# The low half of every weight, made on VectorE or on GpSimd

## The reference

```python
for layer in range(DEPTH):                      # DEPTH = 2
    h = rms_norm(x, mix_norm_g[layer])
    y = hgrn2_mixer(...) if layer % 2 == 0 else mla_mixer(...)
    m = memory_attention(...)
    x = x + concatenate([y, m]) @ w_out[layer]
    x = x + conv_ffn(rms_norm(x, ffn_norm_g[layer]), w_up[layer], ..., w_down[layer])
h = x
h = h + 0.5 * _swiglu(_rmsnorm(h, ffn1_norm), ffn1_w_in, ffn1_w_out)
z = _rmsnorm(h, mix_norm) @ w_in
h = h + concatenate([_conv_module(...), _gla(...)]) @ w_out
h = h + 0.5 * _swiglu(_rmsnorm(h, ffn2_norm), ffn2_w_in, ffn2_w_out)
h = h + sigmoid(_rmsnorm(h, ple_norm) @ ple_w_gate) * (p @ ple_w_proj)
return _rmsnorm(h, final_norm)
```

## Time and profile before

| | |
|---|---|
| median of 3 runs | 1320.73 us |
| span of the profiled execution | 1316.1 us |
| its own time | not on the page; by the median 4.6 us lie around the span |
| TensorE busy | 1248.9 us, 95% |
| VectorE busy | 844.6 us, 64% |
| ScalarE busy | 662.6 us, 50% |
| GpSimd busy | 3.5 us |
| mean granted TensorE clock | 0.978 |

### The profile page before, as it was taken

How to read it: one execution, slowest core, us unless ns; L and a number is a source line. 1 busy time by engine, 2 the same in 40 slices (tenths; PEclk the granted TensorE clock), 3 DMA queues, 4 the chain that set the end, 5 groups by cost and what they waited for, 6 DMA issues and landing times.

```text
span 1316.1 us, 21598 instructions
## 1 busy us (share of the span) xinstructions
PE 1248.9 (95%) x8351; PEld 1140.8 (87%) x8360; DVE 844.6 (64%) x1556; ACT 662.6 (50%) x1156; POOL 3.5 (0%) x9
## 2 busy tenths in 40 slices
PE   6999789999999889999999999999999899999996
PEld 6999768999998667899999799999899679999984
DVE  7877947666667845666766655554778855555563
ACT  6745435555546643555555534443667134344452
POOL 0000000000000000000000000000000000000000
PEclk9999979999999979999999999999999999999998
DMA  8534403554455212255455454455543134444540
GB/s 346 199 134 145 147 30 144 191 191 182 175 188 207 111 49 96 101 201 184 186 191 192 147 207 179 185 191 191 189 148 144 49 120 183 176 178 183 189 144 32
DMA packets 20433, 211.40 MB, mean 161 GB/s; under 512 B 2400, under 2 KB 2400, under 8 KB 3360
## 3 DMA queue, kind: packets, MB, share of 16 engines
q1 hardware_dynamic: 20016, 208.90, 42.9%
q0 software_dynamic: 368, 1.84, 0.4%
HBM read 209.68 MB, written 1.05 MB: 160 GB/s over the span
## 4 chain that ended last, share of the span: by engine, by line
PE 86%; DVE 8%; ACT 4%; issue 1%; DMA 1%; SPq 0%; ACTq 0%; DVEq 0%
PE ps L305 25%; PE ps L306 25%; PE ps L307 25%; PE ps L310 10%; DVE w_lo L1233 2%; ACT w_hi L812 1%; ACT arena L812 1%; DMA raw<-in_stream 1%; ACT arena L847 1%; DVE x L1299 1%; DVE arena L1729 0%; PE ps L633 0%; PE ps L468 0%; DVE arena L1323 0%; DVE arena L1547 0%
## 5 line engine op out<-in xcount | busy, mean ns | idle before, releaser
L1233 DVE TENSOR_TENSOR w_lo<-raw,w_hi 128x1024 fp32r<-128x1024 f32 (+1 forms) x390 | 444.7, 1167 | 41.3 <-ACT w_hi L812 40.6
L305 PE MATMUL ps<-h_hi,w_hi 128*128 128x256 f32 x1608 | 456.0, 284 | 0.2 <-DVE h_lo L1286 0.2
L307 PE MATMUL ps<-h_hi,w_lo 128*128 128x256 f32 x1608 | 455.0, 283 | 0.0
L306 PE MATMUL ps<-h_lo,w_hi 128*128 128x256 f32 x1608 | 455.0, 283 | 0.0
L812 ACT ACTIVATE w_hi<-raw 128x1024 fp32r<-128x1024 f32 (+1 forms) x390 | 379.1, 1007 | 6.0 <-PE ps L307 4.6
L305 PEld LDWEIGHTS ps<-h_hi,w_hi 128*128 128x128 f32 x1608 | 308.3, 192 | 3.5 <-issue 0.3
L306 PEld LDWEIGHTS ps<-h_lo,w_hi 128*128 128x128 f32 x1608 | 308.3, 192 | 3.2
L307 PEld LDWEIGHTS ps<-h_hi,w_lo 128*128 128x128 f32 x1608 | 308.3, 192 | 0.0
L305 PE MATMUL ps<-w_hi,y_hi 128*128 128x512 f32 (+2 forms) x550 | 212.1, 386 | 12.3 <-DVE y_lo L1342 5.0
L306 PE MATMUL ps<-w_lo,y_hi 128*128 128x512 f32 (+2 forms) x550 | 210.4, 382 | 0.0
L307 PE MATMUL ps<-w_hi,y_lo 128*128 128x512 f32 (+2 forms) x550 | 209.3, 381 | 0.0
(11 more groups left out here) (275 smaller groups left out, 1037.9 us busy)
## 6 DMA issues: line engine op xcount, KB each, us to landing
raw<-in_stream SPq DMA_DIRECT2D x130, 1536.0 KB, 6.3
x<-in_x SPq DMA_DIRECT2D x1, 1024.0 KB, 4.9
arena<-in_mem SPq DMA_DIRECT2D x1, 1024.0 KB, 11.9
x<-in_x POOLq DMA_DIRECT2D x1, 1024.0 KB, 5.7
out<-arena SPq DMA_DIRECT2D x4, 256.0 KB, 2.5
vec<-in_vectors SPq DMA_DIRECT2D x1, 893.0 KB, 6.6
arena<-in_final POOLq DMA_DIRECT2D x1, 512.0 KB, 5.6
arena<-in_masks SPq DMA_DIRECT2D x1, 352.0 KB, 12.0
```

The costliest lines, as they stand in the source:

```text
L305: pe.matmul(o, lh, rh, start=start, stop=False, skip_group_check=True)
L306: pe.matmul(o, lh, rl, start=False, stop=False, skip_group_check=True)
L307: return pe.matmul(o, ll, rh, start=False, stop=stop, skip_group_check=True)
L1233: dve.tensor_tensor(w_lo[:, s, a], raw[:, s, a], w_hi[:, s, a], ALU.subtract).then_inc(s_lo, 1)
```

## The change

GpSimd gets a helper `split`, and makes the low part of all 390 pieces in the order of the stream: those of units 0 to 5, then it sets the area of line 287 to zero (for which it waits as before), then those of units 6 to 129. All calls of `lo` and `split` on VectorE go, and with them the arguments `between` and `after` of two helpers. Since GpSimd works its queue in order, the three transfers move to ScalarE's queue: x behind the copy of the queries of the first memory attention, the other two between the sums of squares and the rest of the norm ahead of the last feed-forward part. No wait of TensorE, SyncE or ScalarE on a counter is changed.

```diff
@@ block.gpsimd
             pool.memset(zero[:, :], 0.0).then_inc(sem("zero_set"), 1)
 
+            def split(units):
+                for u in units:
+                    s = u % SLOTS
+                    for p in range(3):
+                        a = extent(u, p)
+                        pool.wait_ge(s_hi, 3 * u + p + 1)
+                        pool.tensor_tensor(w_lo[:, s, a], raw[:, s, a], w_hi[:, s, a],
+                                           ALU.subtract).then_inc(s_lo, 1)
+
+            split(range(0, U_I))
             pool.wait_ge(sem("memT_lo_done"), 2)
             pool.memset(A(4608, HEADS * S), 0.0).then_inc(sem("r_zero"), 1)
-
-            pool.wait_ge(sem("hg_o_ready"), 1)
-            pool.wait_ge(sem("ma_qT_ready"), 1)
-            pool.dma_start(x[:, :, :], x_in).then_inc(sem("x_back"), 16)
-
-            pool.wait_ge(sem("x_done"), 4 * 6)
-            pool.dma_start(ple, ple_in).then_inc(sem("ple_loaded"), 16)
-            pool.dma_start(fin, fin_in).then_inc(sem("fin_loaded"), 16)
+            split(range(U_I, UNITS))
@@ block.scalar
             ma_queries(0)
+            act.dma_start(x[:, :, :], x_in).then_inc(sem("x_back"), 16)
             for h in range(HEADS):
...
             norm_a(6)
+            act.dma_start(ple, ple_in).then_inc(sem("ple_loaded"), 16)
+            act.dma_start(fin, fin_in).then_inc(sem("fin_loaded"), 16)
             norm_b(6, "ffn3")
@@ block.vector
-            def lo(r, u, p):
...
-                dve.wait_ge(s_hi, n if r is None else r * 9 + n)
...
-                dve.tensor_tensor(w_lo[:, s, a], raw[:, s, a], w_hi[:, s, a], ALU.subtract).then_inc(s_lo, 1)
...
-            split(U_F)
             norm_b(0, "mix0")
...
```

More of the change, by code:

```diff
@@ L1223, in link @@
                 dve.wait_ge(s_chain, chain.at(chain.n))
-            def lo(r, u, p):
-                if u >= UNITS:
-                    return
-                n = 3 * u + p + 1
-                dve.wait_ge(s_hi, n if r is None else r * 9 + n)
-                s = u % SLOTS
-                a = extent(u, p) if r is None else slice(p * PIECE, (p + 1) * PIECE)
-                dve.tensor_tensor(w_lo[:, s, a], raw[:, s, a], w_hi[:, s, a], ALU.subtract).then_inc(s_lo, 1)
-            def split(u):
-                for p in range(3):
-                    lo(None, u, p)
             def rsqrt(out_, mean, n, t1, t2, scale=1.0):
@@ L1260, in squares, with norm_a @@
                 return dve.tensor_tensor_reduce(o, i, i, scale, 0.0, ALU.mult, ALU.add, acc)
-            def norm_a(i, between=None):
+            def norm_a(i):
                 if i:
@@ L1278, in norm_a @@
                                       ALU.mult).then_inc(sem("factors_done"), 1)
-                if between:
-                    lo(None, between, 2)
             def norm_b(i, gain):
@@ L1289, in norm_b, with residual @@
                         m.then_inc(sem("hT_ready"), 1)
-            def residual(i, u, scale=1.0, after=None):
+            def residual(i, u, scale=1.0):
                 for b in range(4):
@@ L1300, in residual @@
                                              ALU.mult, ALU.add).then_inc(sem("x_done"), 1)
-                if after:
-                    lo(None, after, 1)
             def ffn(i):
@@ L1336, in body @@
                     dve.tensor_tensor(gg[:, g, :], sa[:, g, :], other, ALU.mult).then_inc(sem("gate_done"), 1)
[L1337 to L1340, removed]
                     dve.wait_ge(sem("g_hi_done"), at(r, n0 + j + 1))
                     dve.tensor_tensor(y_lo[:, g, :], gg[:, g, :], y_hi[:, g, :], ALU.subtract).then_inc(sem("g_lo_done"), 1)
-                    if j < CH - 1:
-                        lo(r, U0 + j + 2, 2)
                 body(None, 0)
@@ L1353, in ffn @@
                     body(None, j)
-                lo(None, U0 + CH + 1, 0)
                 if i < 3:
-                    residual(FFN_NORM[i], U0 + CH, 1.0 if cw else 0.5, U0 + CH + 1)
+                    residual(FFN_NORM[i], U0 + CH, 1.0 if cw else 0.5)
             def head_sums(sq, groups, w):
@@ L1535, in _ @@
             ma_queries(0)
-            split(U_OUT0 + 2)
             for t in range(T):
@@ L1570, in _ @@
             ffn(0)
-            norm_a(2, U_MLA)
+            norm_a(2)
             norm_b(2, "mix1")
-            split(U_MLA + 1)
-            split(U_MLA + 2)
             dve.wait_ge(s_evac, EV[U_MLA])
@@ L1614, in _ @@
             link(dve.tensor_tensor(x2, k4[2], k4[3], ALU.add))
-            split(U_UQ + 2)
             ma_queries(1)
@@ L1705, in _ @@
             ffn(1)
-            norm_a(4, U_FFN2)
+            norm_a(4)
             norm_b(4, "ffn2")
-            split(U_FFN2 + 1)
             ffn(2)
-            norm_a(5, U_IN2)
+            norm_a(5)
             norm_b(5, "mix2")
-            split(U_IN2 + 1)
             link(dve.memset(glu[:, :, 0:TAPS - 1], 0.0))
@@ L1775, in _ @@
             m.then_inc(sem("gla_in_done"), 1)
-            split(U_IN2 + 8)
             conv(30)
@@ L1821, in _ @@
                 m.then_inc(sem("y_ready"), 1)
-            split(U_OUT2 + 2)
             for t in range(T):
@@ L1846, in _ @@
             m.then_inc(sem("pleT_done"), 1)
-            residual(6, U_FFN3 + CH, 0.5, U_PROJ)
-            norm_a(7, U_PROJ)
-            split(U_PROJ + 1)
-            split(U_PROJ + 2)
+            residual(6, U_FFN3 + CH, 0.5)
+            norm_a(7)
             norm_b(7, "ple")
-            split(U_PROJ + 3)
             dve.wait_ge(s_evac, EV[U_PROJ])
```

26 lines of the change are left out of this document (removed).

## The result

The changed kernel takes 1404.81 us (median of 4 runs, 1400.32 to 1405.34) beside 1320.76 us for the kernel before on the same chip: a ratio of 1.063, with a 95% interval from 1.0617 to 1.0644. It is 84 us slower where 16.5 were forecast, and above the range.

The account below looks back on a forecast made before the run. TensorE was taken as the bound, with VectorE on the path only at a few places. Losses of one GpSimd piece per critical chain summed to 16.5 us on 1320.7, giving 1337 us; the 8-in-10 range was 1315 to 1372.

Parts of the forecast that it names:

- What bounds the kernel: Whole kernel: TensorE busy 95% of the span; VectorE has 8% of the last chain, nothing to gain inside feed-forward parts.
- The price of a piece: Low part of 1024 columns on GpSimd: 2.3 us, range 0.93 to 2.79.
- The stream is fast enough: Steady chunks: three pieces take 6.9 us of a chunk's 8.58, so GpSimd keeps up; break-even 2.86 us a piece.
- The moved transfers: Three transfers issued by ScalarE instead of GpSimd: zero cost, at most 0.67 us each without cover.
- The sign: Whole kernel: 3.4 us faster if GpSimd disturbs nobody, a loss if VectorE steps wait for whole remainders of pieces.
- I take the end of a whole piece per critical chain: VectorE's critical chains: each waits for one GpSimd piece, 2.3 us, instead of the gain; 16.5 us lost in sum.
- the third rival: VectorE's inverse roots: a queued piece slips into every gap, chains pay all queued pieces; 45 us, 1366 us, chance 0.15.
- the start: First unit: GpSimd's low parts come late for TensorE, 0.9 us lost, between 0 and 1.8.
- the norms: Behind projections 3.9 us lost, behind first and third feed-forward parts 3.6; other two covered by TensorE's zeros.
- the second mixer: Ahead of its heads: six pieces in two bursts, two waits less TensorE's cover, 4.1 us lost.
- the levels and the third mixer: Only the long convolution was priced: 4.5 us of cover for one piece, so 0.
- reading the first mixer: Reading the first mixer's result: one piece of 2.3 us less a gain of 1.1, so 1.2 us lost.

Follow-up runs that it names:

- the kernel whose VectorE makes the pieces: Against the kernel before, transfers on ScalarE and two unread 400-column GpSimd subtractions per full high part, VectorE keeping all low parts: 1516.68 us (1.1478).

## Why the prediction was wrong, point by point

**What bounds the kernel:** right. VectorE was on the path only at a few places, and there was nothing to gain in the FFN parts.

**The price of a piece:** 2.49 us, forecast 2.3, inside the bounds. The 59 full pieces with no instruction of VectorE beside them have a mean of 2.40 us, the other 311 one of 2.51: part of the price is the turns that GpSimd gives up. Half of what the page "GPSIMD Engine Reference" of the Trainium skill (Elementwise, side-by-side cycle accounting) has for 2048 columns is 2.25, an estimate 6% below the 2.40. On VectorE the forecast compared it with 1167 ns, a mean that mixes in 20 pieces cut short; its 370 full pieces have 1220, so there too the half is some 6% low.

**The stream is fast enough:** right. TensorE waited for GpSimd's `w_lo` once, for 0.6 us, and the FFN parts lost 3.4 us in 755 (forecast 2.8, for the first chunks). The steady chunk was forecast at 0 with two half waits; they are 0.95 and 1.64 us, and covered.

**The moved transfers:** 0, shown by the run with them alone.

**The sign:** right, and for the reason given. The Trainium skill ("SBUF — State Buffer", Who interferes with whom) has the exclusion for whole instructions; the runs agree, with held steps of 2.3, 1.2 and 0.65 us for instructions of 1024, 512 and 256 columns, and VectorE's groups of steps with an operand in PSUM as short in the changed kernel as before (means within 1%). The same section counts one-operand steps in two-port modes with those that are held; the 0.46 us beside memsets agree.

**The step that failed is "I take the end of a whole piece per critical chain".** It is one per step, until the chain or GpSimd's queue ends: six of them, 13.8 us, in the chain of the memory's norm. This was the third rival, every small step waits, put at 0.15; the argument against it, that GpSimd may take longer than the 0.03 us gap between two steps to begin, was wrong: the next piece follows at once and the next step stands behind it. And even that rival, at 1366, was 39 us short, because of a second fault: both sums were made over the chains near which I had found a gain, not over all of VectorE's chains of small steps. By the ledger, forecast against measured:

- the start, 0.9 against 18.5. I asked only when the first unit's pieces were ready. The memory's norm stands right behind it; before the change TensorE had no wait worth a row for its factors, now 9.3 us (L1398), with six of GpSimd's pieces beside it;
- the norms, 7.5 against 22.2. Two were said to have TensorE's zeros as cover. The one behind the second feed-forward part had it (0.1 us lost); the last lost 9.0, with six pieces released in its chain (VectorE's four last steps of the root and two factor steps took 13.9 us for them). Those behind the first and third feed-forward parts lost 3.1 and 3.4 where 1.6 and 2.0 were forecast;
- the second mixer, 4.1 against 20.6. 10.9 of it from the chain ahead of the heads to their end, where the rival had 13.8; 9.7 in the squares and factors ahead of its second projections, with no term;
- the levels and the third mixer, 0 against 5.2 and 9.9. I had looked at one step of the long convolution and not at the filter steps that stand ahead of the linear attention's in VectorE's queue: seven of them took 2.37 to 2.63 us each, where they take 0.41 or 0.48 with no piece beside them, until GpSimd had nothing left;
- reading the first mixer, 1.2 against 7.9.

## What to carry to other kernels

Before work goes to GpSimd, list every stretch in which VectorE's small SBUF steps are waited for, and price each at the smaller of two sums: its steps times one GpSimd instruction, or GpSimd's whole queue there. With very short GpSimd instructions one step can pay the whole queue, so take the queue as the upper bound. VectorE's busy share says nothing about this. Here GpSimd was free only where VectorE had slack, in the FFN bodies, and there was nothing to gain in those; the gain that was had, 7.6 us, came with another order of VectorE's own work.

## What the runs showed of the hardware that was not expected

- The hold goes both ways: GpSimd's subtraction of 400 columns had a mean of 1469 ns in the kernel whose VectorE makes the pieces, and 1061 ns in the 23 cases with no instruction of VectorE beside it. (By the 2.49 us of a piece I had put it at 0.97.)
- A GpSimd instruction has a price of its own beside its columns: with nothing of VectorE beside it a subtraction took 0.737 us for 256 columns, 1.291 for 512 and 2.398 for 1024. The line through these is 2.16 ns a column plus 0.18 us, an estimate from the three.
- The turns are not assured: one step of 128 x 256 on VectorE waited 33 us through 47 GpSimd instructions of 256 columns.
- A set to zero on GpSimd, 434 ns, holds a one-operand TENSOR_SCALAR of two columns on VectorE (0.46 us) and not a two-operand step (0.16 us).
- VectorE's reductions (TENSOR_REDUCE) of SBUF were not held: the five that ran beside a piece in the changed kernel took 686 ns for 512 columns, 407 to 409 for 256 and 286 for 128, as before.
- With the new waits TensorE's mean granted clock fell from 0.978 to 0.948, and its busy time grew by 28.3 of the 87.4 us of longer span.
